# Attention turned around its values, adaLN units moved behind the qkv products, and two of eight update chunks split between ScalarE and GpSimd

## The chip, the cores and the metric

The kernel runs on one core of a Trainium2 chip. The metric is the device time of one execution in microseconds, of which the median of several runs counts. The engines are TensorE (PE, with its weight loads as PEld), VectorE (DVE), ScalarE (ACT), GpSimd (POOL) and SyncE (SP), which here only issues DMAs.

## The reference, cut to what matters

One step of a two-layer trunk over 128 context and 128 latent tokens of width 1024, all in float32. Layer 0 mixes tokens with a convolution module, layer 1 with attention; each is followed by a mixture of 64 experts, of which each token takes 8, and one shared expert. Every sub-layer is normalised, shifted and scaled, and gated by adaLN parameters.

```python
for i in range(DEPTH):                       # DEPTH = 2
    sh1, sc1, g1, sh2, sc2, g2 = split(silu(cond) @ ada_w[i] + ada_b[i], 6)   # for both kinds of tokens
    h = rms_norm(y, norm_mix[i]) * (1 + sc1) + sh1
    m = conv_module(h) if i % 2 == 0 else attention(h)
    y = y + g1 * m
    y = y + g2 * moe(rms_norm(y, norm_ffn[i]) * (1 + sc2) + sh2)

def attention(h):                            # 16 query heads, 4 key/value heads, 64 wide
    q, k, v = split(h @ wqkv);  q, k = rms_norm(q), rms_norm(k)      # latent: also rope2d(q), rope2d(k)
    s = concat([q @ k.T * 64 ** -0.5, sink])     # latent queries see latent and cached context keys (256), context ones 128
    p = softmax(s)[..., :-1]
    return (p @ v) @ wo                          # also out: k and v of the context tokens
```

## The kernel before

Tokens stand in two groups, context (g = 0) and latent (g = 1). The state `yT` holds them turned: eight chunks of 128 features by 256 tokens. Every engine's program is written out by hand, in the order in which it runs, with counted semaphores between engines; no scheduler moves anything.

**The order of a layer.** A mixer, then the loop over 32 pairs of experts (both at once, one on each half of the array), then an update of `yT`. In the loop `gate_up` (L951), `down` (L983) and `combine` (L994) are PE's; SP streams the weights, six experts ahead. Both layers' loops are the same code.

**The update at a loop's end (L1986).** When the last product of the loop is done (`acc_done`), DVE computes for each of the eight chunks and both groups `yT = acc * gate + kept`, where `acc` lies in PSUM and `kept` was read back from DRAM into `hb`. After layer 0 ACT squares each chunk (L1173), PE sums the squares (L626), and the roots and the normalisation of layer 1 follow. After layer 1 PE turns the chunks (L1120), ACT and DVE copy them out of PSUM (L1440, L1991) and SP stores them.

**The qkv part of layer 1.** PE makes six products (L730), three of the latent group and then three of the context group, 512 columns each. Between the first two latent products it computes four of the `ada_w` units (L606: one unit is 128 rows of the adaLN weights times 2048 columns, 1 MB loaded by SP at L403), between the second and third four more. Units 32 to 40 are requested right after the loop of layer 0, behind the 6 MB of `wqkv`; units 41 to 47 wait until the unit before them in the same buffer is used. ACT copies the products out of PSUM (L1301), DVE normalises and rotates (L1615 to L1655), PE turns q and k (L739) and ACT copies them to `qTt`, `kTt` (L1313, L1317).

**Attention.** There are eight steps i of four query heads each: four latent ones over 256 keys, then four context ones over 128 keys. PE computes the scores of two steps at once (`at_scores(m)`, L774). For each step DVE takes the maxima (L1665 to L1673), ACT the exponentials with their sums (L1346), PE turns the probabilities (L786), DVE copies them to `probT` (L1679), PE multiplies them with the values (L800: the probabilities are the stationary operand, the 64 columns of a value head move), and DVE divides by the sum and writes `otok` (L1685 to L1689). `probT` holds one step, and the output one bank, ps6. PE fills in the units 40 to 47 of `ada_w`. After the last step PE turns `otok` (L826), ACT copies it to `oT` (L1359), and `project` (L638) multiplies with `wo`, which is one load of 4 MB in the buffer that held `wqkv`.

**What the loads behind it wait for.** The first experts' weights of layer 1 wait for units of `ada_w` to be used and for steps of `project`: the last of them, the shared expert and the extra buffer, for its end (`pj_out` 8).

Of the kernel before, what the change touches and what calls it, by code (L numbers as in the profile page):

```python
# [23 lines left out]
ALU = mybir.AluOpType  # L24
# [96 lines left out]
def build_kernel(nc, x_prompt, x_sample, cache_k, cache_v, c, c_ctx, ada_w, ada_b, norm_mix, norm_ffn,  # L121
# [4 lines left out]
    with ExitStack() as ctx:  # L126
# [112 lines left out]
        y_back = hb[:, 0:KC * TT].rearrange("p (k t) -> p k t", k=KC)  # L239
        shh = W[:, 2688:3712].rearrange("p (j t) -> p j t", j=4)  # L240
# [53 lines left out]
        def ada_row(e):  # L294

            if e == 0:
                return hb_f[:, 2048:2560]
            return arow[:, e, :] if e < 3 else arow_late
# [5 lines left out]
        otok = ring_f[:, B0 + 3072:B0 + 5120].rearrange("p (g n) -> p g n", g=G)  # L304
# [9 lines left out]
        probT = W[:, 2816:3840].rearrange("p (b n) -> p b n", b=2)  # L314
# [5 lines left out]
        def by_row(bank):  # L320
# [11 lines left out]
        dve_step, act_step = sem("dve_step"), sem("act_step")  # L332
# [21 lines left out]
        at_s, at_max, at_exp, at_pt, at_ptc, at_o, at_on, at_ot, at_otc = (  # L354
            sem("at_s"), sem("at_max"), sem("at_exp"), sem("at_pt"), sem("at_ptc"), sem("at_o"), sem("at_on"),
            sem("at_ot"), sem("at_otc"))
# [37 lines left out]
        def _(sp):  # L394
# [81 lines left out]
            for l in range(L):  # L476
# [20 lines left out]
                else:  # L497
# [5 lines left out]
                    sp.dma_start(wo, attn_wo[0].rearrange("(k p) n -> p k n", p=P)).then_inc(ld_wo, 16)  # L503
# [84 lines left out]
            for h in range(2):  # L588
                for g, y in enumerate((y_prompt, y_sample)):
                    if 2 * h + g < 3:  # L590
                        sp.wait_ge(y_out, 2 * h + g + 1)
                    else:
                        sp.wait_ge(y_ready, L * KC + 1)
# [5 lines left out]
        def _(pe):  # L599
# [30 lines left out]
            def project(w, x, ready, per, loaded, banks):  # L630

                pe.wait_ge(loaded, 16)
                for b in range(4):
                    for h in range(2):
                        for k in range(KC):
                            if b == h == 0:
                                pe.wait_ge(ready, k // per + 1)
# [33 lines left out]
            for l in range(L):  # L671
# [50 lines left out]
                else:  # L722
# [20 lines left out]
                    qkv_product(1, 0)  # L743
                    ada_products(range(EARLY, EARLY + 4), ps[2])
                    qkv_product(1, 1)
                    ada_products(range(EARLY + 4, EARLY + 8), ps[2])
                    qkv_product(1, 2)
                    ada_transposes(4, ps[2])
                    qkv_product(0, 0)
# [29 lines left out]
                    def at_transposes(i):  # L779
                        nk = 1 + HEADS[i][0]  # L780
                        pe.wait_ge(at_exp, i + 1)
                        if i == 2:
                            pe.wait_ge(at_trc, 7)
                        for kk in range(nk):
                            for q in range(QG):
                                mm = pe.transpose(ps[4 + kk][:, q * T:(q + 1) * T],  # L786
# [3 lines left out]
                    def at_values(i):  # L790
                        g, j = HEADS[i]
                        nk = 1 + g
                        pe.wait_ge(at_ptc, i + 1)
# [1247 lines left out]
```

## Time and profile before

| what | value |
|---|---|
| three runs | 1299.8, 1302.45, 1305.2 us (median 1302.45) |
| the profiled execution's own time | 1300.94 us |
| its span | 1299.0 us |
| PE busy | 1267.8 us, 98% |
| DVE, ACT, POOL busy | 440.6, 324.4, 56.8 us |
| the DMA queue that SP fills | 93.4% of 16 engines' span |
| loop of layer 0, on the chain from its first `gate_up` to the update | 185.55 to 655.43 us |
| layer 1 before its loop | 655.43 to 820.68 us |
| loop of layer 1 and the end | 820.68 to 1299.0 us |

A page shows busy time per engine over the whole span. With PE at 98% it says little on the stretches between the loops; there the chain of waits and the timeline of each engine tell what ends last. Times in rows are from the span's start.

### The profile page before, as it was taken

How to read it: one execution, taken by the hardware profiler on the slowest of the kernel's cores; microseconds unless marked ns; L12 is line 12 of the kernel's file. 1: busy time of each engine (PE TensorE's matmuls, PEld its weight loads, DVE VectorE, ACT ScalarE, POOL GpSimd, SP SyncE). 2: the span in 40 equal slices, each digit the busy share in tenths (PEclk: the TensorE clock that was granted, in tenths of full speed). 3: DMA queues.
4: the chain of work that ended last, by engine and by line, in shares of the span. 5: the costliest groups of instructions: out<-in, count | busy, mean ns of one | idle time of the engine just before them, and what ended most of it. 6: DMA issues, size and time to landing. Idle time of an engine off the chain costs nothing.

```text
span 1299.0 us, 18966 instructions
## 1 busy us (share of the span) xinstructions
PE 1267.8 (98%) x7020; PEld 709.7 (55%) x7020; DVE 440.6 (34%) x1503; ACT 324.4 (25%) x718; POOL 56.8 (4%) x86
## 2 busy tenths in 40 slices
PE   6999999999999999999999899999999999999998
PEld 3876775545545454455454578655445444544544
DVE  1696272222222222222235535422222222222223
ACT  3575331121121122112121433112212211221111
POOL 0295000000000000000000000000000000000000
PEclk9999999999999999999999999999999999999999
DMA  9987999999999999999996557699999999999994
GB/s 365 385 324 302 405 401 403 414 419 419 420 420 421 421 420 421 420 419 421 363 413 284 235 227 292 248 403 418 419 420 420 421 420 421 421 421 421 419 419 193
DMA packets 84022, 497.42 MB, mean 383 GB/s; under 512 B 10681, under 2 KB 19553, under 8 KB 27648
## 3 DMA queue, kind: packets, MB, share of 16 engines
q1 hardware_dynamic: 83392, 496.47, 93.4%
q8 instruction: 35, 0.57, 0.2%
q10 hardware_dynamic: 576, 0.22, 0.1%
q14 instruction: 19, 0.16, 0.0%
HBM read 493.26 MB, written 3.41 MB: 382 GB/s over the span
## 4 chain that ended last, share of the span: by engine, by line
PE 85%; DVE 6%; DMA 6%; ACT 2%; SPq 1%; issue 1%; POOL 0%; DVEq 0%; ACTq 0%
PE ps L951 34%; PE ps L983 17%; PE ps L994 9%; PE ps L922 7%; PE ps L638 4%; DVE ps L1574 3%; PE ps L730 3%; DMA ring<-in_conv_w_dram 2%; PE ps L865 2%; DMA ring<-in_ada_w_dram 2%; DMA S<-in_exp_w_up_dram 2%; PE ps L606 1%; PE ps L969 1%; PE ps L906 1%; PE ps L961 1%; SPq L403 1%
## 5 line engine op out<-in xcount | busy, mean ns | idle before, releaser
L951 PE MATMUL ps<-ring,xg 128*64 128x512 f32 x1344 | 296.8, 593 | 0.2
L951 PEld LDWEIGHTS ps<-ring,xg 128*64 128x64 f32 x1344 | 104.6, 137 | 186.8 <-issue 167.9
L951 PE MATMUL ps<-S,xg 128*64 128x512 f32 x704 | 154.8, 592 | 0.3 <-DMA S<-in_exp_w_up_dram 0.3
L983 PE MATMUL ps<-ring,W 128*64 128x512 f32 x672 | 153.5, 598 | 0.0
L1866 DVE TENSOR_TENSOR ypart<-ps,ypart 128x512 fp32r<-128x512 f32 x128 | 88.5, 691 | 179.8 <-ACT ypart L1396 179.8
L1855 DVE SCALAR_TENSOR_TENSOR vec<-silu_h,W,ps 128x256 f32<-128x256 f32 x64 | 30.8, 481 | 333.3 <-ACT silu_h L1390 333.3
L994 PEld LDWEIGHTS ps<-comb,ypart 128*128 128x128 f32 x1024 | 126.3, 190 | 18.6 <-issue 18.6
L994 PE MATMUL ps<-comb,ypart 128*128 128x256 f32 x1024 | 135.2, 285 | 0.0
L1390 ACT ACTIVATE silu_h<-ps 128x256 f32<-128x256 f32 x64 | 24.6, 385 | 407.3 <-PE ps L951 407.3
L1385 ACT ACTIVATE xg<-ps 128x384 f32<-128x384 f32 x176 | 83.3, 492 | 168.1 <-PE ps L922 168.1
L1396 ACT ACTIVATE ypart<-ps 128x512 fp32r<-128x512 f32 x128 | 76.5, 598 | 184.6 <-PE ps L983 184.6
L951 PEld LDWEIGHTS ps<-S,xg 128*64 128x64 f32 x704 | 50.6, 137 | 101.0 <-issue 87.5
L922 PE MATMUL ps<-hot,h_hi 128*128 128x240 f32 x352 | 93.6, 302 | 0.0
L983 PEld LDWEIGHTS ps<-ring,W 128*64 128x64 f32 x672 | 44.5, 136 | 75.0 <-issue 71.9
L922 PEld LDWEIGHTS ps<-hot,h_hi 128*128 128x128 f32 x352 | 67.0, 190 | 32.5 <-issue 32.5
L922 PE MATMUL ps<-hot,h_lo 128*128 128x240 f32 x352 | 83.9, 274 | 0.0
L983 PE MATMUL ps<-S,W 128*64 128x512 f32 x352 | 80.4, 598 | 0.0
L1860 DVE COPY W<-ps 128x256 f32<-128x256 f32 x64 | 27.1, 424 | 119.7 <-PE ps L969 119.7
L922 PEld LDWEIGHTS ps<-hot,h_lo 128*128 128x128 f32 x352 | 66.9, 190 | 0.1
L688 PE MATMUL ps<-hT,ring 128*128 128x256 f32 x256 | 56.3, 381 | 1.2 <-DMA ring<-in_conv_w_dram 1.2
L688 PEld LDWEIGHTS ps<-hT,ring 128*128 128x128 f32 x256 | 48.3, 190 | 10.3 <-issue 1.7
L1574 DVE SCALAR_TENSOR_TENSOR ps<-W,vec,ps 128x256 f32<-128x256 f32 x134 | 53.6, 481 | 0.0
(249 smaller groups left out, 1097.4 us busy)
## 6 DMA issues: line engine op xcount, KB each, us to landing
ring<-in_exp_w_gate_dram SPq DMA_DIRECT2D x86, 1024.0 KB, 15.8
ring<-in_exp_w_up_dram SPq DMA_DIRECT2D x86, 1024.0 KB, 18.4
ring<-in_exp_w_down_dram SPq DMA_DIRECT2D x86, 1024.0 KB, 18.2
S<-in_exp_w_gate_dram SPq DMA_DIRECT2D x44, 1024.0 KB, 16.2
S<-in_exp_w_up_dram SPq DMA_DIRECT2D x44, 1024.0 KB, 19.0
S<-in_exp_w_down_dram SPq DMA_DIRECT2D x44, 1024.0 KB, 18.9
ring<-in_ada_w_dram SPq DMA_DIRECT2D x26, 1024.0 KB, 21.2
S<-in_ada_w_dram SPq DMA_DIRECT2D x22, 1024.0 KB, 14.4
```

Of the source, the lines that this page charges most:

```text
L638: mm = pe.matmul(banks[b][:, h * TT:(h + 1) * TT], w[:, k, (2 * b + h) * P:(2 * b + h + 1) * P], x[:, k, :], start=(k == 0), stop=(k == KC ...
L688: mm = pe.matmul(ps[3 + n % 4][:, h * TT:(h + 1) * TT], w1[:, k, h * D + n * P:h * D + (n + 1) * P], hT[:, k, :], start=(k == 0), stop=(k ...
L730: mm = pe.matmul(ps[3 * g + n][:, :], hT[:, k, g * T:(g + 1) * T], wqkv[:, k, n * 512:(n + 1) * 512], start=(k == 0), stop=(k == KC - 1))
L922: mm = pe.matmul(spanned(bank[:, 0:6 * SLOTS], g), held, spanned(hot[buffer][:, g, :], g), start=(n == 0), stop=(n == 2 * 2 - 1), skip_gro ...
L951: mm = pe.matmul(PGU[64 * b:64 * b + 64, :].rearrange("p (h f) -> p h f", h=2), xg[:, places[k][m], 64 * b:64 * b + 64], gate_up_of(w[b])[ ...
L983: mm = pe.matmul(bank[64 * b:64 * b + 64, :], hidT[:, j, 64 * b:64 * b + 64], down_of(w[b])[:, j, n * 512:(n + 1) * 512], start=(j == 0), ...
L994: mm = pe.matmul(acc[k // 2][:, (k % 2) * TT:(k % 2 + 1) * TT], ypart[:, part, k * P:(k + 1) * P], comb[:, par, :], start=False, stop=Fals ...
L1385: act.activation(blocks, bank[:, 0:2 * SLOTS * pairs].rearrange("p (m s) -> p m s", m=pairs), ACT.Copy).then_inc(act_xg[l], 1)
L1396: act.activation(half_of(0, h), bank[:, :], ACT.Copy).then_inc(act_yhi[l], 1)
L1574: ins = dve.scalar_tensor_tensor(last, x, tap, o, ALU.mult, ALU.add)
L1855: dve.scalar_tensor_tensor(hid, silu_h, wslot[:, par:par + 1], PGU[:, DE:2 * DE], ALU.mult, ALU.mult).then_inc(dve_h[l], 1)
L1866: dve.tensor_tensor(half_of(1, h), bank[:, :], half_of(0, h), ALU.subtract).then_inc(dve_ylo[l], 1)
```

## The change

- **The update at both loops' ends.** DVE keeps chunks 0 to 5. For chunks 6 and 7 ACT multiplies `acc` with the gate into `y_gated` (four instructions of 128 by 128, `gate_y`), and POOL adds `kept` (two of 128 by 256). After layer 0 ACT does this ahead of its squares, after layer 1 ahead of its copies. Who reads chunks 6 and 7 waits on `y_added`.
- **The qkv part.** PE makes the three latent products in a row, then all eight units, then the context ones.
- **Attention.** DVE divides the probabilities by their sum before PE turns them (`scaled`). The turned probabilities of two steps are kept; DVE copies the half over own keys, ACT the half over cached keys (`context_copy`). `at_values(m)` takes two steps at once: the value heads are stationary, 512 turned probabilities move, and the product lands already turned, so that ACT copies it straight to `oT` (`output_copy`). The turn of `otok` and `otok` itself are gone. q and k of the context group are turned right after the first scores instead of after the second step. `project` starts its first four chunks on three of the four output copies. `wo` is loaded in another arrangement, as four loads of 64 partitions each.
- **A place.** The row of the last adaLN third moves from `W` to `hb`, as `probT` grew.

On PE, the qkv part of layer 1 before (L730 a product of 512 columns, L606 units of `ada_w`, L618 their turn, L754 the turn of the cached keys):

```order
L730 MATMUL ps<-S,hT 128x512 x8
L606 MATMUL ps<-ring,scT 32x512 x16
L730 MATMUL ps<-S,hT 128x512 x8
L606 MATMUL ps<-ring,scT 32x512 x16
L730 MATMUL ps<-S,hT 128x512 x8
L618 MATMUL ps<-cst,W 128x128 x4
L730 MATMUL ps<-S,hT 128x512 x16
L754 MATMUL ps<-cst,ring 128x128 x2
L730 MATMUL ps<-S,hT 128x512 x8
```

and of the changed kernel (L738, L614, L626 and L760 are the same four):

```order
L738 MATMUL ps<-S,hT 128x512 x24
L614 MATMUL ps<-ring,scT 32x512 x32
L738 MATMUL ps<-S,hT 128x512 x8
L626 MATMUL ps<-cst,W 128x128 x4
L738 MATMUL ps<-S,hT 128x512 x8
L760 MATMUL ps<-cst,ring 128x128 x2
L738 MATMUL ps<-S,hT 128x512 x8
```

All eight units stand behind the third latent product now, and their turn behind the first context product.

On PE, the first three steps of attention before, from the first scores on (L774 scores, L606 units, L786 turned probabilities, L800 values, L739 turned q and k of the context group):

```order
L774 MATMUL ps<-W 128x256 x8
L606 MATMUL ps<-ring,scT 32x512 x12
L786 MATMUL ps<-cst,hb 128x128 x8
L774 MATMUL ps<-W 128x256 x8
L800 MATMUL ps<-ring,W 128x64 x8
L786 MATMUL ps<-cst,hb 128x128 x8
L606 MATMUL ps<-ring,scT 32x512 x4
L800 MATMUL ps<-ring,W 128x64 x8
L739 MATMUL ps<-cst,ring 128x128 x10
L786 MATMUL ps<-cst,hb 128x128 x8
L774 MATMUL ps<-W 128x128 x8
L800 MATMUL ps<-ring,W 128x64 x8
```

and of the changed kernel (L780 scores, L747 turned q and k, L614 units, L795 turned probabilities, L810 values):

```order
L780 MATMUL ps<-W 128x256 x8
L747 MATMUL ps<-cst,ring 128x128 x10
L614 MATMUL ps<-ring,scT 32x512 x12
L795 MATMUL ps<-cst,hb 128x128 x8
L780 MATMUL ps<-W 128x256 x8
L795 MATMUL ps<-cst,hb 128x128 x8
L614 MATMUL ps<-ring,scT 32x512 x4
L810 MATMUL ps<-W,ring 64x512 x4
L795 MATMUL ps<-cst,hb 128x128 x8
L780 MATMUL ps<-W 128x128 x8
L795 MATMUL ps<-cst,hb 128x128 x8
L614 MATMUL ps<-ring,scT 32x512 x4
```

The value products stand once per two steps, as four matmuls with 512 moving columns instead of sixteen with 64, and the turn of q and k has moved ahead of the first probabilities.

On DVE, the same place of the changed kernel, from the second maxima on (L1699 to L1707 maxima, L1721 to L1723 the division of the probabilities, L1715 their copy):

```order
L1707 TENSOR_SCALAR ring<-ring 128x4
L1721 TENSOR_TENSOR ring<-ring 128x4
L1722 RECIPROCAL ring<-ring 128x4
L1723 TENSOR_TENSOR hb<-hb,ring 128x1024
L1721 TENSOR_TENSOR ring<-ring 128x4
L1722 RECIPROCAL ring<-ring 128x4
L1723 TENSOR_TENSOR hb<-hb,ring 128x1024
L1715 COPY W<-ps 128x512
L1699 TENSOR_REDUCE ring<-ps 128x2 x2
```

Where one division of a 128 by 256 output per step stood behind the value product (L1689), one of 128 by 1024 probabilities now stands ahead of the turn.

The core of the diff:

```diff
+        y_gated = hb[:, KC * TT:(KC + 2) * TT].rearrange("p (k t) -> p k t", k=2)
-        probT = W[:, 2816:3840].rearrange("p (b n) -> p b n", b=2)
+        probT = W[:, 2816:4864].rearrange("p (b k n) -> p b k n", b=2, k=2)
+        TURNED = [2 * (i + 1) if i < NKV else NKV + i + 1 for i in range(2 * NKV)]
...
-                    sp.dma_start(wo, attn_wo[0].rearrange("(k p) n -> p k n", p=P)).then_inc(ld_wo, 16)
+                    for j in range(NKV):
+                        b = j % 2
+                        sp.dma_start(wo[HD * b:HD * b + HD, QG * (j // 2):QG * (j // 2 + 1), :],
+                                     attn_wo[0, QG * HD * j:QG * HD * (j + 1), :].rearrange("(q d) n -> d q n", d=HD)
+                                     ).then_inc(ld_wo, 16)
...
                     def at_transposes(i):
-                        pe.wait_ge(at_exp, i + 1)
-                        if i == 2:
+                        pe.wait_ge(at_on, i + 1)
+                        if i == 0:
                             pe.wait_ge(at_trc, 7)
+                        else:
+                            pe.wait_ge(at_ptc, TURNED[i - 1 if i <= NKV else i - 2])
...
+                    def at_values(m):
+                        g = HEADS[2 * m][0]
                         nk = 1 + g
+                        pe.wait_ge(at_ptc, TURNED[2 * m + 1])
+                        if m >= 1:
+                            pe.wait_ge(at_otc, m)
+                        for kk in range(nk):
+                            for b in range(2):
+                                j = HEADS[2 * m + b][1]
...
+                                mm = pe.matmul(ps[6][HD * b:HD * b + HD, :], v, probT[:, b, kk, :],
...
+                    for m in range(NKV):
+                        at_transposes(2 * m)
+                        if m + 1 < NKV:
+                            at_scores(m + 1)
+                        at_transposes(2 * m + 1)
+                        ada_products([EARLY + 12 + m], ps[7])
+                        at_values(m)
                     ada_transposes(5, ps[7])
-                    project(wo, oT, at_otc, 2, ld_wo, AB)
+                    project(wo, oT, at_otc, 4, ld_wo, AB, 3, NKV)
...
+            def gate_y(l):
+                act.wait_ge(acc_done, l + 1)
+                for k in range(KC - 2, KC):
+                    for g in range(G):
+                        ins = act.activation(y_gated[:, k - KC + 2, g * T:(g + 1) * T],
+                                             acc[k // 2][:, (k % 2) * TT + g * T:(k % 2) * TT + (g + 1) * T],
+                                             ACT.Identity, scale=mod[:, l, g, 5 * KC + k:5 * KC + k + 1])
+                    ins.then_inc(y_scaled, 1)
...
+                    qk_copies(0, [ps[4], ps[5], ps[6]])
+                    exps(0)
+                    for m in range(NKV):
+                        exps(2 * m + 1)
+                        if m < NKV // 2:
+                            context_copy(2 * m)
+                            context_copy(2 * m + 1)
+                        if m + 1 < NKV:
+                            exps(2 * m + 2)
+                        else:
+                            ada_copy(5, ps[7])
+                        output_copy(m)
...
+            for l in range(L):
+                pool.wait_ge(y_moved, 32 * (l + 1))
+                for k in range(2):
+                    pool.wait_ge(y_scaled, 2 * l + k + 1)
+                    pool.tensor_tensor(yT[:, KC - 2 + k, :], y_gated[:, k, :], y_back[:, KC - 2 + k, :], ALU.add
+                                       ).then_inc(y_added, 1)
...
+                    for m in range(NKV):
+                        scaled(2 * m)
+                        scaled(2 * m + 1)
+                        prob_copy(2 * m)
+                        if m + 1 < NKV:
+                            maxima(2 * m + 2)
+                        prob_copy(2 * m + 1)
+                        if m + 1 < NKV:
+                            maxima(2 * m + 3)
...
-                for k in range(KC):
+                for k in range(KC - 2):
                     for g in range(G):
                         v, kept = yT[:, k, g * T:(g + 1) * T], y_back[:, k, g * T:(g + 1) * T]
```

## Rows read from the trace of the kernel before

**Rows 1.** The page's chain that ended last: shares of the span by engine.
```profile
PE 85%; DVE 6%; DMA 6%; ACT 2%; SPq 1%; issue 1%; POOL 0%; DVEq 0%; ACTq 0%
```

**Rows 2.** Chain between the loops, 640 to 800 us: start us, us, what.
```profile
676.22 7.06 PE ps L730 x16
...
694.35 13.73 PE ps L730 x32
...
717.39 2.02 PE ps L774 x16
...
721.44 1.82 ACT hb L1346 x8
...
725.23 3.68 PE ps L774 x16
...
760.95 27.63 PE ps L638 x128
```

**Rows 3.** Timeline, 640 to 700 us: start us, us, instructions, idle before and releaser.
```profile
655.43 4.22 DVE L1986 SCALAR_TENSOR_TENSOR yT<-ps,mod,hb 128x128 f32<-128x128 f32 x16 [0.83 <-PE ps L1059]
...
656.07 4.03 ACT L1173 ACTIVATE hb<-yT 128x256 f32<-128x256 f32 x8 [0.42 <-DVE yT L1986]
...
656.54 5.46 PE L626 MATMUL ps<-hb,cst 128*128 128x256 f32 x16 [0.84 <-ACT hb L1173]
...
671.48 2.78 PE L606 MATMUL ps<-ring,scT 128*32 128x512 f32 x24
...
675.15 1.06 PE L606 MATMUL ps<-ring,scT 128*32 128x512 f32 x8 [0.89 <-DMA ring<-in_ada_w_dram]
```

**Rows 4.** Groups by form, 640 to 800 us: busy us, mean ns | idle before.
```profile
L1679 DVE COPY W<-ps 128x512 f32<-128x512 f32 x12 | 7.9, 684 | 5.6 <-PE ps L786 5.6
...
L1346 ACT ACTIVATE hb<-ps,ring 128x128 f32<-128x128 f32 x16 | 5.6, 360 | 0.0
...
L1665 DVE TENSOR_REDUCE ring<-ps 128x2 f32<-128x512 f32 x8 | 5.1, 682 | 4.0 <-PE ps L774 4.0
...
L1665 DVE TENSOR_REDUCE ring<-ps 128x2 f32<-128x256 f32 x8 | 3.0, 416 | 1.5 <-PE ps L774 1.5
...
L1359 ACT ACTIVATE hT<-ps 128x512 f32<-128x512 f32 x4 | 2.1, 602 | 1.8 <-PE ps L826 1.8
...
L1687 DVE RECIPROCAL ring<-ring 128x4 f32<-128x4 f32 x8 | 1.4, 178 | 0.3
...
L1620 DVE TENSOR_TENSOR ring<-ring 128x1024 f32<-128x1024 f32 x1 | 1.2, 1224 | 0.0
```

**Rows 5.** Engines' busy time by stretch; the third number from the end is the granted clock.
```profile
723.00:725.20 2.20, 1.09 (x8) 0.86 (x8) 0.76 (x2) 2.18 (x11) 0.00 (x0) 1.00 1.02 398
725.20:729.00 3.80, 3.77 (x17) 2.71 (x18) 0.57 (x2) 0.00 (x0) 0.00 (x0) 0.55 1.04 393
```

**Rows 6.** Chain of the last 15 us: start us, us, what.
```profile
1290.67 4.24 DVE yT L1986 x16
...
1294.96 0.45 PE ps L1120 x2
```

**Rows 7.** POOL's groups of the whole span: busy us, mean ns | idle before.
```profile
L1453 POOL TENSOR_TENSOR W<-W,hb 128x256 f32<-128x256 f32 x30 | 21.7, 725 | 57.3 <-ACT hb L1224 57.3
```

**Rows 8.** DVE beside POOL (L1574) and without (L1855): ns min/median/max, first and last start.
```profile
L1574 DVE SCALAR_TENSOR_TENSOR ps<-W,vec,ps x105: 477/480/484, 49.8 to 99.5; 128x256 f32<-128x256 f32 x105
...
L1855 DVE SCALAR_TENSOR_TENSOR vec<-silu_h,W,ps x64: 479/481/483, 193.5 to 1274.5; 128x256 f32<-128x256 f32 x64
```

**Rows 9.** DMA issues, 640 to 800 us: count, KB each, median us to landing.
```profile
ring<-in_ada_w_dram SPq DMA_DIRECT2D x16, 1024.0 KB, 21.2
...
S<-in_attn_wo_dram SPq DMA_DIRECT2D x1, 4096.0 KB, 13.2
```

**Rows 10.** Chain of the whole span, one `down` of the loop: start us, us, what.
```profile
836.17 3.58 PE ps L983 x16
```

**Rows 11.** PE's timeline near the end of layer 1's loop: start us, us, idle before.
```profile
1266.97 7.09 PE L951 MATMUL ps<-S,xg 128*64 128x512 f32 x32 [0.34 <-DMA S<-in_exp_w_up_dram]
```

More of the change, by code:

```diff
@@ L628, in sum_squares, with project @@
                     mm.then_inc(ss_ready, 1)
-            def project(w, x, ready, per, loaded, banks):
-                pe.wait_ge(loaded, 16)
+            def project(w, x, ready, per, loaded, banks, first=1, loads=1):
+                pe.wait_ge(loaded, 16 * loads)
                 for b in range(4):
@@ L741, in qk_transposes @@
                             mm.then_inc(at_tr, 1)
[L743 to L747, printed above, removed]
+                    for n in range(3):
+                        qkv_product(1, n)
+                    ada_products(range(EARLY, EARLY + 8), ps[2])
+                    qkv_product(0, 0)
                     ada_transposes(4, ps[2])
-                    qkv_product(0, 0)
                     qkv_product(0, 1)
@@ L1127, in _ @@
         def _(act):
-            steps = [0]
-            def step(ins):
-                steps[0] += 1
-                ins.then_inc(act_step, 1)
-                act.wait_ge(act_step, steps[0])
             def cols(v):
@@ L1167, in load_table @@
                 act.activation(spare[:, 1:2], spare[:, 0:1], function)
+            def gate_y(l):
[6 more added lines that the diff above has]
+                    ins.then_inc(y_scaled, 1)
             def squares(src, n, ready, value, bank=7):
                 load_table(ACT.Sqrt)
+                if ready is y_ready:
+                    gate_y(0)
                 for k in range(KC):
-                    act.wait_ge(ready, value(k))
+                    if ready is y_ready and k >= KC - 2:
+                        act.wait_ge(y_added, k - KC + 3)
+                    else:
+                        act.wait_ge(ready, value(k))
                     act.activation(sq[:, k, :], src[:, k, :], ACT.Square).then_inc(sq_ready, 1)
@@ L1695, in _ @@
                     maxima(0)
                     maxima(1)
-                    for i in range(G * NKV):
-                        prob_copies(i)
-                        if i + 2 < G * NKV:
-                            maxima(i + 2)
-                        outputs(i)
+                    for m in range(NKV):
[7 more added lines that the diff above has]
+                            maxima(2 * m + 3)
```

108 lines of the change are left out of this document (44 added, 64 removed).

## Prediction

> **What bounds the kernel now.** I read the page first: PE is busy 98% of the span, and the chain that ended last is PE's for 85% [rows 1]. So the two expert loops, some 930 of 1299 us, are PE's own work, and the change doesn't touch their instructions. What it touches are three places where PE waits for others or idles, and I read each from the chain of waits and the engines' timelines. First, the qkv part of layer 1: three units of `ada_w` run without a break from 671.48, the fourth starts at 675.15 after a wait for its load [rows 3]. Second, attention, from the first scores at 717.39 to the first product of `project` at 760.95 [rows 2]: 43.56 us in which the end is handed from PE to DVE to ACT and back at every step. Third, the updates at both loops' ends: sixteen DVE instructions in 4.22 and 4.24 us [rows 3, 6], with PE waiting at the second one.
>
> **The weights of the second loop** could take a gain back, so I looked there next. Near its end PE waits once for a load, 0.34 us [rows 11]: DMA just keeps up. But the last loads ahead of that loop (shared expert, extra buffer) are asked for when `project` ends, and the later ones when a buffer comes free in the loop, so the stream moves with PE. What is gained ahead of `project`'s end, I let stand in full.
>
> **The qkv part.** With the three latent products in a row the units stand 14 us later, when their loads have landed. Before, four units took from 671.48 to 676.22; at 2.78/3 = 0.93 each they need 3.7 [rows 2, 3], so the wait is worth 1.0. Two products in a row take 13.73, two apart 2 x 7.06 [rows 2], so a join saves up to 0.39; there are two joins now and there was one, which gives 0.2. Together -1.2. DVE's normalising and rotating of the latent group starts some 9 us earlier, but it hid behind context products before, too, so this gives nothing. Units 41 to 47 can be asked for only when unit 32 is used, at about 686 instead of 672.4 (671.48 + 0.93); at 21.2 us to landing [rows 9] the three that come first are there by 710, and PE wants them at 719 or later: 9 us of cover, past which each us counts in full.
>
> **The update after layer 0.** ACT now multiplies four 128 by 128 pieces before its first square. The nearest row is the exponential of that size out of PSUM, 0.36 [rows 4], so 1.2 for four that overlap a little; from 655.5, when DVE starts, that puts ACT's first square some 0.6 later than 656.07. PE's sums start later by as much. They are what ends last there: 5.46 us of sums run to 662.0, while the squares end at 660.1 [rows 3]. So the end moves by +0.5. The lower bound is -0.4, if the sums followed the squares, since DVE is done 1.06 earlier; the upper one +0.7. POOL's two adds at 0.73 [rows 7] are done by about 657.7, ahead of the last two squares.
>
> **The update after layer 1.** DVE keeps 12 of 16 instructions at 0.265: -1.06 [rows 6]. Behind its last one PE had two turns (0.45), and has six now, since the turns of chunks 6 and 7 stand behind that of chunk 5: +0.45 at 0.11 a turn. That is -0.6. ACT's four pieces end before its first copy is due, and POOL's adds at about 1290.7 + 0.7 + 2 x 0.73 = 1292.9, one us before DVE's last; each us that they take longer than that counts.
>
> **Attention.** Here I laid the new order out instruction by instruction, each engine in its order, each instruction at its row's duration, 0.04 from one engine to the next (1294.91 to 1294.96 in rows 6). Laid out so, the order of before gives 43.6 from the first scores to `project`, where the trace has 43.56, so the method carries. Durations: a pair of latent scores 2.0 at full clock [rows 2]; the maxima of a latent step 1.76 (two reductions at 0.68 and three small steps of 0.16 to 0.18), of a context step 1.2 (two at 0.42); a latent step's exponentials 1.9 (eight entries in 1.82 and a small one) [rows 2], a context step's 1.5 (four at 0.36); a division of 128 by 1024 as the 1.22 of L1620 and two small steps, 1.65, for context 1.1; copies 0.68 on DVE, 0.60 on ACT [rows 4]; eight turns 1.1 [rows 5]. The new value product has the form of `down`: 16 entries of 512 columns in 3.58 [rows 10], so 1.8 for a latent pair's eight and 0.9 for a context pair's four; before, each step had 2.0 or 1.1. From the first scores' start it goes:
> - scores to 2.0, first maxima to 3.8; ACT copies the turned q and k until 4.7, then both steps' exponentials to 8.6.
> - Pair 0: step 0 is divided by 8.4 and turned by 9.5, the next scores end at 11.4, step 1 is turned by 12.4, DVE's copy waits behind the maxima of step 2 and ends at 13.8, values to 15.7, output copy to 16.3.
> - Pair 1: exponentials of step 3 (queued on ACT behind that output copy) to 18.3, division to 20.0, copy to 20.6, turns to 21.7, exponentials of step 4 to 23.8, output copy to 25.0.
> - Pair 2: exponentials of step 5 to 26.6, division to 27.7, maxima of step 6 to 29.4, its exponentials to 31.1, output copy to 31.7.
> - Pair 3: exponentials of step 7 to 33.3, division to 34.4, turns to 35.0, the last unit to 35.9, values to 36.8, the turn of the adaLN row to 37.2. `project` starts there; its second four chunks come 0.9 later, when the last output copy has ended.
>
> So 37.2 at full clock: -6.4. The waits that the change adds are in this: PE's turn behind DVE's division, ACT's exponentials behind the output copy. What goes is the division behind the values, the turn of the output with its copies, and half of the value products' time.
>
> **The clock.** The granted clock was full at 723 to 725.2, where PE did 1.09 us of turns in 2.2, and 0.55 in the next 3.8 us, when the second scores ran [rows 5]: 1.2 GHz most of that time, and they took 3.68 instead of 2.02 [rows 2]. Laid out without this, before comes to 42.1. The new order has thinner places: PE has nothing from 5.9 to 8.4, just ahead of the second scores, and only two half turns from 31 to 35. I take a fall to half at both. The first puts the second scores at 3.65 and `project` 1.7 later. The second lies on step 7's turn, the last unit, the last values and the first of `project`, 0.5 + 1.0 + 0.9 and some, of which I count 1.3. That makes 40.2, or **-3.3**. The ends are -6.4 (no fall) and -1.7 (four falls).
>
> **The sum.** -1.2 + 0.5 - 3.3 - 0.6 = -4.6. The profiled execution took 1300.94, so its like would be 1296.3; it lies 1.5 under the median of three, and the mean of all four known times is 1302.1. I take that as the base: **1297.5**.
>
> **Rivals.**
> - *The clock holds in attention*, or falls where PE is not on the path. For it: through the thin stretch itself the clock was still full [rows 5]. Against it: the fall came right behind it, and the new gaps are wider. Then -1.2 + 0.5 - 6.4 - 0.6 = -7.7: 1294.4.
> - *More falls, or longer handovers.* With four falls attention gives 1.7 and the sum is -3.0: 1299.1.
> - *The weights' stream ends layer 1's loop, not PE.* For it speaks the one wait of 0.34 [rows 11]. Then all but the 0.6 at the end is waited away: 1301.5. Against it: the stream starts with `project`'s end.
> - *POOL's adds hold DVE up.* If DVE stood still during both adds, the end would lose 1.46: -3.1, 1299.0. In the convolution DVE's update of the same kinds of operands takes 480 ns beside POOL and 481 without [rows 8], which speaks against it. The Trainium skill (GPSIMD Engine Reference, section 8, Key points) says that GpSimd shares its SBUF interfaces with VectorE and contends with VectorE instructions that have two SBUF inputs; the update would be one if the gate's column counted beside `kept`. L1574 has such a column, too, and shows nothing of it.
> - *Slower: `wo` lands late.* Four loads into 64 partitions each replace one that landed in 13.2 [rows 9]. They are asked for about when the first scores start, and `project` wants them some 42 us later. From 3.2 times the 13.2 on, each us is lost; from 4.0 times (53 us) the kernel is slower by over 0.5%. At five times (66 us) it would lose 24 and end at 1321.5. Against it: the bytes and the 4 KB rows are the same.
>
> **How the numbers follow.** A measurement of this kernel can tell about 0.5% from no change, 6.5 us. I give the forecast 0.53, the holding clock 0.21, more falls 0.10, the stream 0.07, POOL 0.05, `wo` 0.04. Only the holding clock and part of the forecast's spread come out below 1295.6: faster 0.27. Slower is `wo` alone: 0.04. Same has 0.69. The range takes in the holding clock with a little of the runs' spread, and the stream's case up to 1301: 1293.5 to 1301.
>
> **What would show it.** The profile after should have no wait for `ada_w` in the qkv part; 40 us (37 to 42) from the first scores to `project`; a half-clock stretch at the second scores; 3.2 us of DVE updates at the end, with POOL done before DVE; no PE wait for `wo`. I would be wrong if the first sums of layer 1 ended much later, if PE waited for units 41 to 43, or if the waits for loads in the second loop grew by what attention gave.

## The result, and the profile after

| | before | after |
|---|---|---|
| median of four runs each | 1302.16 us (1299.80 to 1305.20) | 1293.97 us (1292.37 to 1295.08) |
| the profiled execution, its span | 1300.94, 1299.0 us | 1293.72, 1291.9 us |
| PE, DVE, ACT, POOL busy | 1267.8, 440.6, 324.4, 56.8 us | 1257.9, 440.9, 328.1, 59.6 us |

The ratio is 0.9937, with a 95% interval from 0.9916 to 0.9958: 8.2 us, 0.63% faster. The range held the time. The likeliest case, 1297.5 and no difference that can be told, did not come; the time lies at the rival in which the clock holds in attention, 1294.4.

The chain of waits of the changed kernel between the loops, which answers to [rows 2, 3] (start us, us, what; L634 sums of squares, L738 products of qkv, L614 units, L780 scores, L646 `project`):

```profile
657.33 5.36 PE ps L634 x16
...
665.37 20.60 PE ps L738 x48
685.98 7.00 PE ps L614 x64
...
716.66 2.00 PE ps L780 x16
...
725.37 1.95 PE ps L780 x16
...
753.88 27.63 PE ps L646 x128
781.51 3.47 PE ps L634 x16
```

The three latent products stand without a break, the eight units too, and no load is waited for. From the first scores to `project` it is 37.22 us where it was 43.56, and the second scores take 1.95 where they took 3.68. The granted clock of the same execution (third number from the end; the first pair behind the comma is PE's busy time):

```profile
656.00:661.00 5.00, 3.67 (x9) 2.98 (x10) 2.92 (x12) 3.75 (x12) 1.41 (x2) 0.66 1.02 406
716.00:736.00 20.00, 15.71 (x130) 8.89 (x122) 15.05 (x38) 13.69 (x48) 0.00 (x0) 1.00 1.03 208
736.00:754.00 18.00, 12.47 (x86) 5.60 (x87) 12.11 (x39) 9.10 (x42) 0.00 (x0) 1.00 0.89 353
```

Attention ran at 2.4 GHz throughout. The first sums of squares of layer 1 ran mostly at 1.2 GHz: that is why they took 5.36, where the same sixteen products behind `project` took 3.47. The 5.46 of before [rows 3] was such a number, too, and I had not seen it. The same window of the kernel before:

```profile
656.00:661.00 5.00, 4.46 (x13) 3.50 (x14) 3.66 (x15) 3.33 (x8) 0.00 (x0) 0.66 1.03 409
```

and the sums behind `project` in its chain:

```profile
788.58 3.47 PE ps L626 x16
```

The end, which answers to [rows 6], from the chain:

```profile
1284.13 3.20 DVE yT L2021 x12
...
1287.38 0.89 PE ps L1120 x6
...
1288.29 0.69 DVE ring L2026
```

and POOL's adds beside DVE's update, from the timeline of all engines:

```profile
1284.13 3.19 DVE L2021 SCALAR_TENSOR_TENSOR yT<-ps,mod,hb 128x128 f32<-128x128 f32 x12 [0.84 <-PE ps L1056]
...
1284.90 1.41 POOL L1488 TENSOR_TENSOR yT<-hb 128x256 f32<-128x256 f32 x2 [626.88 <-ACT hb L1166]
```

POOL is done one us before DVE, as reckoned. Between the two profiles the 7.1 us of span come from these places, by the timeline's starts: the end of layer 0's loop +0.30, from there to the first scores -1.03, attention -6.34, `project` 0.00, from its end to the last update +0.53, the end -0.56.

### The profile page after: what moved, and what is told of

It is laid out like the page before. It is cut to its first block, busy times and chain, and to the rows that moved or that the text cites. A ratio compares the mean times of both kernels' runs of the same rounds, so it can differ in the third digit from the quotient of the medians.

```text
span 1291.9 us, 18801 instructions
## 1 busy us (share of the span) xinstructions
PE 1257.9 (97%) x6932; PEld 697.8 (54%) x6932; DVE 440.9 (34%) x1491; ACT 328.1 (25%) x730; POOL 59.6 (5%) x90
## 4 chain that ended last, share of the span: by engine, by line
PE 87%; DVE 6%; DMA 4%; ACT 2%; issue 1%; SPq 1%; ACTq 0%
PE ps L948 34%; PE ps L980 17%; PE ps L991 10%; PE ps L919 7%; PE ps L646 4%; DVE ps L1608 4%; PE ps L738 3%; DMA ring<-in_conv_w_dram 2%; PE ps L862 2%; DMA S<-in_exp_w_up_dram 2%; PE ps L614 2%; PE ps L966 1%; PE ps L903 1%; PE ps L634 1%; PE ps L958 1%; PE ps L842 1%
## 5 line engine op out<-in xcount | busy, mean ns | idle before, releaser
L1488 POOL TENSOR_TENSOR yT<-hb 128x256 f32<-128x256 f32 x4 | 2.8, 727 | 1168.2 <-ACT hb L1166 1168.2
```

## The experiments

All were timed beside the kernel before on the same chip; its medians in the three groups of runs were 1301.51 (26 runs), 1301.64 (30) and 1301.77 (21). Every run also left a profile, and these turned out to say more than the medians. The kernels of this table are explained below it; where a text says "the changed kernel" with a difference in us, its second set of runs is meant, 1293.55. The table is read from PE's and DVE's timelines, by the starts of the first instructions: A from DVE's update after layer 0 to the first scores, B from there to `project` (0.16 less than by the chain), C from DVE's update after layer 1 to the end of the span (which is given to 0.1). The last column has the work at half clock, or its us, from A on.

| kernel | A | B | C | at half clock |
|---|---|---|---|---|
| before | 61.96 | 43.40 | 8.33 | first sums; second scores |
| before_sums_kept | 61.96 | 43.10 | 8.38 | 754 to 757 |
| before_filled | 62.14 | 43.72 | 8.35 | 736 to 740 |
| before_kept_fit | 63.83 | 42.27 | 8.38 | 677 to 680 |
| update_alone | 61.82 | 49.84 | 7.81 | 739 to 760 |
| attention_alone | 61.92 | 37.07 | 8.35 | none |
| units_back | 61.89 | 38.66 | 7.74 | 753 to 756 |
| qkv_alone | 59.39 | 44.93 | 8.51 | 736 to 743; last turns |
| attention_old | 59.29 | 43.87 | 7.79 | second scores; 734 to 738 |
| update_old | 59.38 | 39.30 | 8.53 | 747 to 754; last turns |
| after | 60.93 | 37.06 | 7.77 | first sums |
| after_again | 59.29 | 39.71 | 8.28 | 748 to 755; last turns |
| after_kept | 60.47 | 38.83 | 8.98 | none |
| after_kept_fit | 59.29 | 37.06 | 7.75 | none |

### The changed kernel once more

No edit.

> The changed kernel once more, for a second profile of it. Theory (the clock fell in the kernel before because PE was thin ahead of the second scores, and the changed order isn't thin enough there): second scores 2.0 us again, 37.2 us from the first scores to project, some 8 us less than the kernel before. Rival (a fall comes or not by where the thin stretch happens to stand in time): second scores 3.65 in some profiles, attention 38.9 then.

1293.55 us (1291.69 to 1296.23, 7 runs), ratio 0.9925 (0.9899 to 0.9951). The second scores took 2.00 again, but the profile is another one: the first sums ran at full clock, and a fall came at the end of attention (windows, as above).

```profile
656.00:661.00 5.00, 3.66 (x18) 3.15 (x19) 3.02 (x12) 3.85 (x13) 1.41 (x2) 1.00 1.02 404
...
735.00:748.00 13.00, 9.11 (x64) 4.08 (x64) 9.22 (x33) 7.85 (x39) 0.00 (x0) 1.00 0.87 334
748.00:755.00 7.00, 5.90 (x21) 2.30 (x22) 2.27 (x5) 1.54 (x3) 0.00 (x0) 0.52 0.74 311
```

The last turn, the last unit, the last values and the start of `project` lie in it, and B is 2.65 longer. The last turns, too, ran slowly: eight in 2.07 in this run's chain of the end.

```profile
1285.12 2.69 DVE yT L2021 x10
...
1287.85 2.07 PE ps L1120 x8
```

So the theory fails at its 37.2, and the rival is right in the main: one and the same order of work has the fall at one place in one execution and at another in the next. The rival's own sign, slow second scores, did not come; what decides where the fall lands is not shown.

### One part undone

The update by DVE alone:

```diff
-                for k in range(KC - 2):
+                for k in range(KC):
                     for g in range(G):
                         v, kept = yT[:, k, g * T:(g + 1) * T], y_back[:, k, g * T:(g + 1) * T]
```

with `gate_y`, POOL's adds and the waits on `y_added` gone.

> The changed kernel with the update as it was: DVE alone, 16 instructions at both loops' ends. Theory: after layer 0 the sums start 0.8 us behind the loop's last product instead of 1.3 and end 0.4 earlier; at the end DVE takes 4.24 instead of 3.20 and two turns stand behind it instead of six, 0.6 later. Together 0.2 slower than the changed kernel, not to be told from it. Rival (POOL's adds hold DVE up, or the split gives more than it seems): 1 us or more away from the changed kernel to either side.

1293.73 us (1291.71 to 1295.70, 8 runs), ratio 0.9931 (0.9908 to 0.9955): 0.2 from the changed kernel in the median, as the theory says, but not quite by its terms. With the clock full at the sums in both, A is 59.38 against 59.29, so the split saves 0.09 after layer 0 instead of costing 0.4. At the end C is 8.53 against 8.28, both with the last turns at half clock.

The units between the latent products again:

```diff
-                    for n in range(3):
-                        qkv_product(1, n)
-                    ada_products(range(EARLY, EARLY + 8), ps[2])
+                    qkv_product(1, 0)
+                    ada_products(range(EARLY, EARLY + 4), ps[2])
+                    qkv_product(1, 1)
+                    ada_products(range(EARLY + 4, EARLY + 8), ps[2])
+                    qkv_product(1, 2)
+                    ada_transposes(4, ps[2])
                     qkv_product(0, 0)
-                    ada_transposes(4, ps[2])
```

with ACT's and DVE's order to match.

> The changed kernel with the eight units of ada_w between the latent products again, as before. Theory: PE waits 0.9 to 1.0 us for the fourth unit's load, and the time from the first latent product to the first scores is 1.2 to 1.5 us longer, as is the whole. Rival (the stream of the second loop's weights sets the end): that time is longer, but the whole is not; PE's waits for loads in the second loop shrink by as much.

1296.68 us (1293.74 to 1298.95, 12 runs), ratio 0.9953 (0.9936 to 0.9970): 3.1 slower than the changed kernel, twice what I expected. PE's timeline shows two waits where the kernel before had one [rows 3] (start us, us, what, idle before and its releaser):

```profile
658.05 3.72 PE L634 MATMUL ps<-hb,cst 128*128 128x256 f32 x16 [1.34 <-ACT hb L1182]
...
664.29 7.03 PE L738 MATMUL ps<-S,hT 128*128 128x512 f32 x16
671.25 1.92 PE L614 MATMUL ps<-ring,scT 128*32 128x512 f32 x16
673.59 1.06 PE L614 MATMUL ps<-ring,scT 128*32 128x512 f32 x8 [0.41 <-DMA ring<-in_ada_w_dram]
676.09 1.07 PE L614 MATMUL ps<-ring,scT 128*32 128x512 f32 x8 [1.44 <-DMA ring<-in_ada_w_dram]
```

The sums ran at full clock here, PE came to the units earlier, and waited 1.85 us for them instead of 0.89. The fourth unit starts 19.65 us behind the start of the update (676.09 - 656.44); in the kernel before it was 19.72 (675.15 - 655.43). The load sets this point, not PE: in the seven profiles with the old place of the units it lies 19.58 to 19.93 behind the start of the update. The chain of the kernel before shows it outright, at a line that does not stand in [rows 2]: from the loop of layer 0 to the fourth unit it holds no work of PE, only the issue of loads and then that unit's own load, under way 2.33 us before the update starts.

```profile
653.10 22.01 DMA ring<-in_ada_w_dram
```

In the table A is 61.8 to 62.1 in six of the seven kernels with the old place of the units, with the first sums slow or fast, and 59.3 to 59.4 in the five with the new place whose sums ran at full clock and were not held up by filling.

The kernel before with the new update and the new place of the units:

```diff
+                    for n in range(3):
+                        qkv_product(1, n)
+                    ada_products(range(EARLY, EARLY + 8), ps[2])
...
-                for k in range(KC):
+                for k in range(KC - 2):
```

with `at_scores` to `project` as before.

> The kernel before with the new update and the new place of the units, but with its own attention and its one load of wo. Theory: the first scores 0.7 earlier than in the kernel before, then 43.6 us to project with the second scores at half clock (3.65), the end 0.6 shorter: 1.3 less than the kernel before, 6.4 more than the changed one. Rival (the fall comes by the place in time): the second scores take 2.0, attention 42.1.

1298.12 us (1295.70 to 1302.37, 12 runs), ratio 0.9968 (0.9950 to 0.9985): 3.4 less than before, where 1.3 was expected, and 4.6 more than the changed kernel, where 6.4 was. The second scores were slow (3.46), and B is 43.87. The first sums ran at full clock, and with no load to wait for that reached the first scores: A is 59.29.

### One part alone

Only the units' new place:

```diff
-                    qkv_product(1, 0)
-                    ada_products(range(EARLY, EARLY + 4), ps[2])
-                    qkv_product(1, 1)
-                    ada_products(range(EARLY + 4, EARLY + 8), ps[2])
-                    qkv_product(1, 2)
+                    for n in range(3):
+                        qkv_product(1, n)
+                    ada_products(range(EARLY, EARLY + 8), ps[2])
...
```

> The kernel before with nothing changed but the place of the eight units behind the three latent products. By the prediction's sum: no wait for units, 1.2 less. Theory now: with the wait gone the first scores follow the sums, so they come 1.2 earlier than before (62.0 from the update) where the clock falls at the sums, and 2.6 to 2.8 where it holds; 2 to 3 less in the median.

1299.02 us (1296.71 to 1300.18, 12 runs), ratio 0.9974 (0.9962 to 0.9987): 2.6 less than before, more than twice the 1.2 that I had booked. A is 59.39 (timeline of DVE and PE; L772 scores):

```profile
655.74 4.22 DVE L1983 SCALAR_TENSOR_TENSOR yT<-ps,mod,hb 128x128 f32<-128x128 f32 x16 [0.84 <-PE ps L1057]
...
715.13 2.00 PE L772 MATMUL ps<-W 64*128 64x256 f32 x16
```

Only the attention and the loads of `wo`:

```diff
-                    project(wo, oT, at_otc, 2, ld_wo, AB)
+                    project(wo, oT, at_otc, 4, ld_wo, AB, 3, NKV)
```

with `at_transposes`, `at_values`, `scaled`, `prob_copy`, `context_copy` and `output_copy` of the change.

> The kernel before with the new attention and the four loads of wo, and nothing else of the change. Theory: 62.0 from the update to the first scores as before, 37.1 to 39.7 from there to project, as the clock holds or falls: 4 to 6 less than the kernel before. Rival (parts don't add up, since the second loop's loads set the end): the time up to project falls by that, the whole by less than 3.

1296.52 us (1295.13 to 1297.12, 5 runs), ratio 0.9964 (0.9951 to 0.9978): 5.3 less than before. In its profile the clock held in attention, and B is 37.07 (PE's timeline; L781 scores, L645 `project`):

```profile
717.69 2.00 PE L781 MATMUL ps<-W 64*128 64x256 f32 x16
...
754.76 27.79 PE L645 MATMUL ps<-hT,S 128*128 128x256 f32 x128
```

What attention gains ahead of `project` arrives at the end nearly whole: B is 6.33 shorter than in the profile of before, the span 5.7. From the first scores to `project` PE's value products take 6.03 us where they took 12.41, and the turn of the output, 1.96, is gone; PE's idle time there grows from 7.3 to 9.7, of which 6.0 are waits of the turns for DVE's division, which now stands ahead of them. How much each part of attention's change gives by itself was not run.

Only the update:

```diff
-                for k in range(KC):
+                for k in range(KC - 2):
```

with `gate_y` and POOL's adds.

> The kernel before with the new update at both loops' ends alone. Theory: whatever it does at the sums after layer 0 is taken by the wait for the fourth unit, 62.0 from the update's start to the first scores; at the end 0.5 to 0.6 less: 0.5 less in all, not to be told from the kernel before. By the prediction's sum: +0.5 - 0.6, the same. Rival (POOL or ACT gets in DVE's way): 1 or more slower.

1300.82 us (1298.95 to 1308.37, 11 runs), ratio 0.9997 (0.9981 to 1.0013): not to be told from before. A is 61.82 and C 7.81, as expected. Its profile happened to be of an execution of 1308.37 us, and shows how bad the clock can get in the old attention (windows, then PE's timeline; L776 scores, L802 values):

```profile
740.00:759.00 19.00, 19.00 (x100) 14.65 (x98) 8.71 (x30) 4.80 (x27) 0.00 (x0) 0.50 0.00 1
```

```profile
739.26 1.97 PE L776 MATMUL ps<-W 64*128 64x128 f32 x16 [0.85 <-ACT hb L1358]
741.16 3.67 PE L802 MATMUL ps<-ring,W 128*128 128x64 f32 x16
```

For 19 us the clock stayed at 1.2 GHz while PE's records show it busy all the time. The same values took 2.00 at full clock.

By the medians the three parts alone give 5.3 + 2.6 + 1.0 (8.8 before rounding), undone one by one 4.6 + 3.1 + 0.2, 7.9, where the whole gave 8.2 and, in the run again, 8.0. So the parts add up, as far as the medians tell: the update's 1.0 and 0.2 can't be told from nothing, and its 0.6 at the end is seen in the profiles alone.

### The clock held by filling

PE multiplies ones that nobody reads where it idles. First the kernel before, ahead of the first sums, and in a second run around the first turn of probabilities:

```diff
                 if l == 1:
+                    keep_clock(ps[1], 12)
                     sum_squares(4, 0)
```

> The kernel before with 12 products of ones ahead of the first sums of squares of layer 1, so that the clock holds there. Theory (the load of the fourth unit of ada_w sets the first scores in the kernel before): the sums take 3.7 to 4.3 instead of 5.46, the first latent product starts 1.2 to 1.5 earlier, PE's wait for units of ada_w grows from 0.9 by as much, and the time from the update to the first scores stays 62.0: no difference in the whole. Rival (the wait is a delay that moves with PE): the first scores 1.2 to 1.5 earlier, and the whole.

1301.36 us (1299.15 to 1304.29, 12 runs), ratio 0.9995 (0.9982 to 1.0008). This one does not test what it should. Twelve products took 2.92 us, not 1.4: each is two entries of 0.12 in the trace, and I had counted one. The sums ran fast (3.62) but started 1.8 later behind the update, and the first latent product came 9.02 behind the update, as before (9.09). That the wait takes up what comes earlier is shown by units_back instead, and by the next run.

```diff
                     for i in range(G * NKV):
+                        if i == 0:
+                            keep_clock(ps[6][:, 256:512], 10)
                         at_transposes(i)
+                        if i == 0:
+                            keep_clock(ps[6][:, 256:512], 6)
```

> The kernel before with 10 products of ones ahead of the first turn of probabilities and 6 ahead of the second scores, where PE was idle 1.2 and 0.8. Theory (thin PE ahead of the second scores lets the clock fall): second scores 2.0 instead of 3.7 and 42.0 from the first scores to project, if no fall comes later in attention; 1.5 less than the kernel before. Rival (the fall comes from elsewhere): second scores 3.5 or more, no difference.

1301.68 us (1300.80 to 1304.89, 12 runs), ratio 1.0002 (0.9989 to 1.0016): no difference. The second scores took 2.00, as the theory says, but the filling was too long again and put them 1.44 later, and a fall came at 736 instead, at the turn of q and k. Its sums happened to run fast (4.32), the first latent product came 7.94 behind the update instead of 9.09, and the first scores came at 62.14: nothing of it was left.

Then the changed kernel at three places, with too much filling:

```diff
+                    FILLS = (12, 0, 9, 0, 4, 0, 8, 8)
...
                     def at_transposes(i):
                         nk = 1 + HEADS[i][0]
+                        if FILLS[i]:
+                            pe.wait_ge(at_exp, i + 1)
+                            keep_clock(ps[2 * (i % 2)], FILLS[i])
                         pe.wait_ge(at_on, i + 1)
```

and 12 products each ahead of the first sums and of the last turns.

> The changed kernel with products of ones that nobody reads on PE in its idle stretches: 12 (1.4 us) ahead of the first sums of squares of layer 1, 4 to 12 ahead of five of the eight turns of probabilities, each only once that step's exponentials are done, and 12 ahead of the last turns. Theory (falls of the clock come behind thin stretches, now here, now there, and cost the changed kernel up to 1.6 us at the sums, 2.5 in attention and 0.5 at the end): no half-clock stretch left at these three places; sums 3.7, 37.1 us from the first scores to project, 7.8 from the last update's start to the end of the span; 1 to 2 us less than the changed kernel in the median. Rival (the filling holds the turns up, or the falls don't come from thinness): the stretches stay, or attention grows past 38.

1295.72 us (1295.06 to 1296.07, 7 runs), ratio 0.9951 (0.9932 to 0.9969): 2.2 slower than the changed kernel, but no half-clock stretch from the sums on, and the seven runs lie within 1.0 us. The loss is the filling's length: against after_kept_fit below, which differs by shorter filling alone, A, B and C are 1.2, 1.8 and 1.2 longer. The one ahead of the sums (PE's timeline, L621 filling, L634 the first sums):

```profile
656.58 2.92 PE L621 MATMUL ps<-cst 128*128 128x128 f32 x24
659.34 3.62 PE L634 MATMUL ps<-hb,cst 128*128 128x256 f32 x16
```

The same cut to size, with 6, 4, 1, 4 and 4 ahead of the turns, 5 ahead of the sums, 3 ahead of the last turns:

> As after_kept, with the products of ones cut to the idle times: a product takes 0.243 us there, so 5 (1.2 us) ahead of the first sums, 6, 4, 1, 4 and 4 ahead of the turns of steps 0, 2, 4, 6 and 7, and 3 ahead of the last turns. Theory: no half-clock stretch from the first sums on, so sums 3.7, 37.1 us from the first scores to project, 7.8 at the end, a spread of about 1 us between runs, and a median of 1291.5 to 1292.5, 1 to 2 less than the changed kernel. Rival (less filling doesn't hold the clock): half-clock stretches in attention and at the end as in the changed kernel, and its median and spread.

1292.10 us (1291.96 to 1292.53, 5 runs), ratio 0.9931 (0.9917 to 0.9945). The profile is as the theory says: sums 3.72, B 37.06, C 7.75. The median is 1.5 below that of the changed kernel's second set of runs and 1.9 below its first, but the ratio beside the kernel before, 0.9931, lies between the changed kernel's two, 0.9925 and 0.9937, so what is shown is that the runs lie closer together, not that it is faster. Windows of it:

```profile
656.00:661.00 5.00, 4.88 (x28) 4.27 (x28) 2.86 (x12) 3.69 (x12) 1.42 (x2) 1.00 1.02 405
715.00:735.00 20.00, 17.87 (x143) 11.30 (x144) 15.76 (x39) 12.96 (x46) 0.00 (x0) 1.00 1.03 210
735.00:752.00 17.00, 14.77 (x102) 7.48 (x103) 11.32 (x37) 8.80 (x41) 0.00 (x0) 1.00 0.89 357
```

And the kernel before in the same way, 3 ahead of the sums, 4 and 3 around the first turn, 3 ahead of the turns of steps 2 and 6 and of the last turns:

```diff
+                        if i in (2, 6):
+                            pe.wait_ge(at_exp, i + 1)
+                            keep_clock(ps[0], 3)
                         at_transposes(i)
```

> The kernel before with products of ones cut to its idle times: 3 ahead of the first sums of squares of layer 1, 4 and 3 around the first turn of probabilities, 3 ahead of the turns of steps 2 and 6, 3 ahead of the last turns. Theory: the clock holds at the sums, but the load of the fourth unit still sets the first scores, 62.0 from the update; second scores 2.0, and 42.0 from the first scores to project where no fall comes in what was not filled; 1 to 1.5 less than the kernel before. Against after_kept_fit, what the change gives without the clock: 2.6 + 5.0 + 0.5, some 8.

1300.21 us (1299.55 to 1303.46, 11 runs), ratio 0.9983 (0.9968 to 0.9997): 1.6 less than before. In attention the clock held, and B is 42.27. The profiled execution is the slowest of the eleven: a fall came behind the waits for the units, at 677 to 680, and A was 63.83. Against after_kept_fit the change is worth 8.1.

## Why the prediction was right, and where it was not

The range and most of the mechanisms held. The sum was 3.6 short: three of its terms were mis-sized, two of them by more than 1 us, and that the range held is in part luck, as the sum behind these terms shows.

**The qkv part, booked at -1.2.** The wait went, as said. But I priced it by its 0.89 in the profile, as if it were a delay that PE carries along. It was a point in time, some 19.7 us behind the update, and whatever PE did faster ahead of it was waited away. With it gone the first scores follow the sums. The profile's sums were slow (5.46), and by the profiles of after and before I would have been nearly right: 60.93 against 61.96. In the eight other profiles without filling ahead of the sums these ran at full clock, and there A goes from 61.9 to 59.3. The term is -2.6, and qkv_alone measured it.

**The clock, booked at +3.1 within attention's -3.3.** I took the fall at the second scores for a property of the order: thin work, then a fall, and thinner work, so two falls. The runs show that a fall lands here or there. In the old attention without filling it came at the second scores in two of five profiles and elsewhere in the other three; in the new one at the place that I named second, the last turns and values, in three of five, never at the one that I named first, and not at all in two. The error was to book falls of 3.0 us in the new order against the one of 1.5 in the row of before (43.56). Like against like, at full clock, is 42.1 laid out and 42.27 measured against 37.2 and 37.07: -5. Over five profiles each without filling the middle ones are 43.87 and 38.66, -5.2, and the run with attention alone has -5.3: these middle ones lie some 1.8 and 1.5 above the walks at full clock. The fall is common to both kernels. Filling took 1.6 from the median of before, just clear of noise, and 1.5 to 1.9 from that of after, which is not clear of it. The laid-out walk itself, 37.2 for 37.22 in the first profile, was right to the rounding.

**The update after layer 0, booked at +0.5.** It is +0.4 where the sums are slow (first latent product 9.48 behind the update, 9.09 before) and -0.1 where they run at full clock (7.84 and 7.85 against 7.94), since then the sums follow the squares. That is the mechanism of the lower bound, -0.4, at a quarter of its size, and the more frequent case: eight of the ten profiles without filling ahead of the sums.

**The update after layer 1, booked at -0.6.** C goes from 8.33 to 7.77, and without a fall there it lies at 8.33 to 8.38 with DVE alone and at 7.74 to 7.81 with the split (after_kept's 8.98 has the too long filling in it): right.

With the measured terms, -2.6 - 0.1 - 5.2 - 0.6 = -8.5 against 8.2 in the runs. The rival of the holding clock, -7.7, was near for a mixed reason: its attention at full clock took a milder case than the usual one and was 1.2 too large, its qkv part was 1.4 too small and its update after layer 0 0.6 too dear. These errors offset each other by luck, and the time lies only 0.5 above the range's lower end, 1293.5; the second set of runs, 1293.55, lies on it.

**The other rivals.** The stream of weights does not end layer 1's loop. PE waits once, 0.8 us where it was 0.34 [rows 11]:

```profile
PE ps L948 <- DMA S<-in_exp_w_up_dram: 0.8, 1, 0.8
```

From the sums behind `project` to the last update all fourteen profiles have 501.7 to 503.1, and the time does not go by how early `project` starts: update_alone, which reached it 13.7 us later behind the update than after did, has 502.69, after 502.78. So the 0.5 that the first pair of profiles loses there is not shown to come from the change. `wo` landed in 15.0 instead of 13.2, far from the 3.2 times from which it would count, and PE did not wait for it:

```profile
S<-in_attn_wo_dram SPq DMA_DIRECT2D x4, 1024.0 KB, 15.0
```

POOL does not hold DVE up: DVE's update took as long per instruction beside POOL's adds as it did alone (minimum, median, maximum in ns, of after, then of before).

```profile
L2021 DVE SCALAR_TENSOR_TENSOR yT<-ps,mod,hb x24: 337/340/351, 655.7 to 1287.0; 128x128 f32<-128x128 f32 x24
```

```profile
L1986 DVE SCALAR_TENSOR_TENSOR yT<-ps,mod,hb x32: 340/343/351, 655.4 to 1294.6; 128x128 f32<-128x128 f32 x32
```

The contention that the Trainium skill (GPSIMD Engine Reference, section 8, Key points) states does not show in this pair, whether or not the gate's column counts as an SBUF input.

## What to carry to other kernels

A wait for a load that was asked for at a fixed point hides everything that gets faster ahead of it, so taking it away is worth the wait and what it hid; read when the load lands, not how long the engine stood. Compare a row with another of the same form before a sum rests on it: sixteen sums in 5.46 and, behind `project`, in 3.47 in the trace of before say that something held the first up; the granted clock of their stretch, 0.66, says what, and before_filled shows what they take there at full clock, 4.32 in step with the squares. Where the granted clock falls in the profile, price both kernels with it and both without, and don't take a fall of the one profile for a property of the order.

## What the runs showed of the hardware

The half clock does not come with the order of the work alone. Of the ten profiles without filling ahead of the first sums of layer 1 it fell there in two; of the ten without filling in attention it fell there in eight, early, in the middle or at the end, and held in two (after and attention_alone). In the three with filling at several places of attention it held; in before_filled, with filling at the first turn alone, it fell later. The Trainium skill (TensorE: Matmul & The Clock Gate, Part 1) says that the gate's measuring runs free and does not start with the kernel, so that one kernel shows a different number of slow products from run to run. The traces here agree that it differs between runs of one kernel, as after and after_again show, and show the same in the middle of a kernel; that the running free is the reason, no run here shows. The spread of the changed kernel's runs, 1291.69 to 1296.23, shrank to 1291.96 to 1292.53 when PE's idle stretches were filled. What I had not expected is how long a fall can last: from 739 to 760 us in update_alone, with PE busy by its records in all of the 19 us shown. Why the clock did not come back sooner there, and whether the new attention is safe from such a stretch, is open: its longest here was 748 to 755.
